# Delta rule's triangular inverse: 8x8 diagonal blocks solved by forward substitution on VectorE, heads planned as three interleaved lists, and the B and C pieces moved in between

## The chip, the cores and the metric

The kernel runs on one core of one Trainium2 chip. The metric is the device time of one execution in microseconds (us). The engines are called by the profile's names: PE is TensorE, PEld its weight loads, DVE VectorE, ACT ScalarE, POOL GpSimd, SP SyncE (here it only issues DMAs).

## What is computed

Two layers of a hybrid trunk on 1024 frames of width 1024, all in fp32. Each layer normalizes x, projects it once, sends the columns to three groups of heads (gated DeltaNet, Mamba-2 SSD, retention), projects their outputs back and adds. The change is in the DeltaNet group (4 heads of 128). The part of the reference that matters, for one chunk:

```
a_low = einsum('bihd,bjhd->bhij', k * beta, k) * decay * strict      # strictly lower triangular
sol   = triangular_solve(a_low + eye, [v * beta, k * beta * exp(gcum)], lower=True)
v_new = u - w @ S                      # u, w: the two halves of sol
o     = (q * exp(gcum)) @ S + ((q @ k.T) * decay) @ v_new
S     = S * exp(glast) + (k * exp(glast - gcum)).T @ v_new
```

The kernel takes chunks of 128 frames instead of 64 and so needs the inverse of a 128x128 unit triangular matrix for every chunk and head.

## The kernel before, in words

**Work and its parts.** The sequence is cut in halves of 512 frames (`HALF`); with two layers this makes four parts (`p` = 0 to 3, `PARTS`), each of four chunks (`NT`). In a part the input projection runs over 26 pieces of 256 columns (`PIECES`), each in two halves. A half is eight TensorE slices; products are taken in three fp32r passes (w_hi with hT_hi, w_low with hT_hi, w_hi with hT_lo), so a slice is three 512-wide matmuls for the pieces that pass through the convolution (`gdn`, `bc`, `sx`) and six 256-wide ones for the gates and the retention pieces. In parts 0 and 2 the weights are loaded and split into their high and low part on the chip (ACT L1954, POOL L2231) and kept in HBM; parts 1 and 3 load the split copies.

**The inverse.** For each head `h` the kernel forms aT (the scaled Gram matrix times the decay, for four chunks at once), starts from X = I minus the pairs on the diagonal (`gdn_gram`: three passes of DVE over 512 columns, L1675 to L1677), and then doubles the size of the inverted diagonal blocks in levels 1 to 6. A level takes `gdn_p` (PE: aT times X; DVE L1713: mask) and `gdn_xx` (PE: XT times the masked product; DVE L1698, or L1701 in the last level: subtract), each in two steps `j` of two chunks. Levels 2 to 5 also transpose X on DVE (L1707). A matmul with fp32 operands shows as two records of PE.

**The recurrence.** `gdn_s`, `gdn_v`, `gdn_o` then walk over the four chunks with the state (L1721, L1726, L1736), and `gdn_fin1` to `gdn_fin3` normalize and gate the output. After the four heads come SSD (two groups) and retention (four heads), and the output projection in units (`out`).

**The order.** Nothing is dynamic: `make_plan` plays a clock forward with costs written by hand (`LINE` 224 ns for a 128-wide fp32 matmul, `SLICE` 705 ns, and so on) and writes one list of steps; each engine runs its instructions in the order of that list, behind semaphores. The planner draws from one list of mixing steps (`mixing_steps`: one head wholly after another, SSD, retention), one of projection steps (`front_steps`), the output units, and short side chains. A mixing step is put in when it is due; otherwise a projection slice fills PE. What may come when is in `known` and `frees`: the convolved columns of a head lie in one of two slots, and the pieces of head h + 2 may only be projected when `gdn_gram` of head h has read its slot.

**Buffers.** `wk` holds 12 tiles of 128x512; X, XT and PP (the masked product, which also serves as oq) are one tile each. PSUM: two banks for the projection, five in a ring for the mixing steps (`MIX_BANKS`), one for outputs.

## Time and profile before

| | us |
|---|---|
| median of 3 runs | 2177.64 |
| lowest, highest | 2175.47, 2180.8 |
| span of the profiled execution | 2179.0 |
| PE busy in it | 2125.8 (98%) |
| PEld, DVE, ACT, POOL busy | 1963.9, 1350.4, 887.6, 482.6 |

The profile gives the span of the profiled execution, from its first to its last instruction, and no separate time of that execution; the span lies inside the spread of the three runs, 1.4 us above their median. A busy share is an average over the whole span, and matmul records overlap each other, so PE's busy time is an upper mark of its work, and what a matmul costs in a full stream is read from the distance of the starts.

### The profile page before, as it was taken

The numbers are of one execution on the slowest core, as the hardware profiler recorded it, in microseconds if no ns is written. First come the engines' busy times: TensorE is split into PE (matmuls) and PEld (weight loads), VectorE is DVE, ScalarE is ACT, GpSimd is POOL, SyncE is SP. The second block draws the span as 40 slices with busy tenths as digits, with TensorE's granted clock in tenths as the row PEclk, the third lists the DMA queues.
The fourth block names the chain that finished last, engine by engine and source line by source line (L and its number), as shares of the span: only waits on it lengthen the run. The fifth ranks groups of instructions, "written<-read, shape, count | busy, mean of one in ns | idle before, by whom it ended". The sixth has DMA issues, their size and how long they took to land.

```text
span 2179.0 us, 39125 instructions
## 1 busy us (share of the span) xinstructions
PE 2125.8 (98%) x15396; PEld 1963.9 (90%) x15396; DVE 1350.4 (62%) x2692; ACT 887.6 (41%) x1779; POOL 482.6 (22%) x432
## 2 busy tenths in 40 slices
PE   7899999999999999999999999999999999999997
PEld 6788988999898898999989899899988988899997
DVE  5777767545578757624567776674556777564334
ACT  5445377332433345402353444763324333562011
POOL 3334332431000011100333334423300000110001
PEclk9999999999999999999999999999999999999999
DMA  6646465666533446544574447666764333583433
GB/s 241 202 161 229 170 225 190 225 227 253 196 136 113 139 155 228 198 155 157 184 248 163 177 175 269 227 229 242 251 214 162 119 116 127 183 279 134 156 138 146
DMA packets 98197, 410.88 MB, mean 189 GB/s; under 512 B 11168, under 2 KB 12256, under 8 KB 84192
## 3 DMA queue, kind: packets, MB, share of 16 engines
q1 hardware_dynamic: 97440, 407.98, 53.0%
q8 instruction: 124, 2.03, 0.4%
q10 hardware_dynamic: 576, 0.41, 0.1%
q14 instruction: 57, 0.47, 0.1%
HBM read 257.18 MB, written 151.16 MB: 187 GB/s over the span
## 4 chain that ended last, share of the span: by engine, by line
PE 75%; issue 3%; DVE 2%; ACT 2%; DMA 1%; POOL 0%; POOLq 0%; DVEq 0%; ACTq 0%
PE ps L1216 71%; PE ps L1219 3%; ACT wk L2105 1%; DMA wo_loaded<-in_w_out 0%; DMA wk<-cum_rows 0%; ACT L2044 0%; DVE slot L1594 0%; DVE acc L1813 0%; DVE wk L1672 0%; ACT wk L2107 0%; ACT wk L2096 0%; DVE wk L1675 0%; DVE wk L1743 0%; ACT wo_hi_odd L1979 0%; DVE wk L1676 0%
## 5 line engine op out<-in xcount | busy, mean ns | idle before, releaser
L1216 PE MATMUL ps<-w_hi,hT_hi 128*128 128x256 f32 x1792 | 526.2, 294 | 4.2 <-POOL w_low L2231 2.5
L1216 PE MATMUL ps<-w_low,hT_hi 128*128 128x256 f32 x1792 | 505.0, 282 | 0.0
L1216 PE MATMUL ps<-w_hi,hT_lo 128*128 128x256 f32 x1792 | 502.7, 281 | 0.0
L2231 POOL TENSOR_TENSOR w_low<-w_loaded,w_hi 128x512 fp32r<-128x512 f32 x208 | 285.7, 1392 | 429.8 <-ACT w_hi L1954 429.5
L1216 PEld LDWEIGHTS ps<-wk 128*128 128x128 f32 x2336 | 309.1, 191 | 51.5 <-issue 15.4
L1216 PE MATMUL ps<-wk 128*128 128x128 f32 (+2 forms) x2336 | 342.7, 282 | 9.6 <-DVE wk L1677 5.8
L1216 PEld LDWEIGHTS ps<-w_hi,hT_hi 128*128 128x128 f32 x1792 | 338.8, 189 | 9.3 <-POOL w_low L2231 4.0
L1216 PEld LDWEIGHTS ps<-w_low,hT_hi 128*128 128x128 f32 x1792 | 338.5, 189 | 2.9 <-issue 2.6
L1216 PEld LDWEIGHTS ps<-w_hi,hT_lo 128*128 128x128 f32 x1792 | 338.6, 189 | 0.0
L1216 PE MATMUL ps<-hT_hi,w_hi 128*128 128x512 f32 x768 | 331.1, 431 | 2.1 <-POOL w_low L2231 2.0
L1216 PE MATMUL ps<-hT_lo,w_hi 128*128 128x512 f32 x768 | 303.2, 395 | 0.0
L1216 PE MATMUL ps<-hT_hi,w_low 128*128 128x512 f32 x768 | 302.2, 393 | 0.0
L1216 PE MATMUL ps<-wo_parts,mixT_hi 128*128 128x256 f32 x960 | 272.6, 284 | 0.0
L1594 DVE SCALAR_TENSOR_TENSOR slot<-raw,par,slot 128x512 f32<-128x512 f32 x240 | 205.1, 857 | 29.9 <-ACT slot L2022 15.7
L1813 DVE TENSOR_TENSOR acc<-acc,ps 128x512 f32<-128x512 f32 x96 | 65.8, 687 | 236.3 <-PE ps L1216 236.0
L1216 PEld LDWEIGHTS ps<-wo_parts,mixT_hi 128*128 128x128 f32 x960 | 182.9, 191 | 3.5 <-issue 2.4
L1216 PEld LDWEIGHTS ps<-hT_lo,w_hi 128*128 128x128 f32 x768 | 144.9, 189 | 33.2
L1216 PEld LDWEIGHTS ps<-hT_hi,w_hi 128*128 128x128 f32 x768 | 146.1, 190 | 24.8 <-POOL w_low L2231 3.8
L1216 PEld LDWEIGHTS ps<-hT_hi,w_low 128*128 128x128 f32 x768 | 146.2, 190 | 20.8 <-issue 1.4
L1216 PE MATMUL ps<-wo_hi_odd,mixT_hi 128*128 128x256 f32 x480 | 141.7, 295 | 12.3 <-DVE wo_parts L1799 8.4
L1954 ACT ACTIVATE w_hi<-w_loaded 128x512 fp32r<-128x512 f32 x208 | 120.8, 620 | 60.1 <-DMA w_loaded<-in_w_in 60.1
L1216 PE MATMUL ps<-wo_hi_odd,mixT_lo 128*128 128x256 f32 x480 | 137.5, 287 | 0.0
(205 smaller groups left out, 3566.7 us busy)
## 6 DMA issues: line engine op xcount, KB each, us to landing
w_loaded<-in_w_in SPq DMA_DIRECT2D x104, 512.0 KB, 5.1
w_split<-w_hi SPq DMA_DIRECT2D x52, 1024.0 KB, 8.1
w_split<-w_low SPq DMA_DIRECT2D x52, 1024.0 KB, 10.1
w_hi<-w_split SPq DMA_DIRECT2D x104, 512.0 KB, 6.3
w_low<-w_split SPq DMA_DIRECT2D x104, 512.0 KB, 7.2
wo_loaded<-in_w_out SPq DMA_DIRECT2D x32, 512.0 KB, 4.2
wk<-cum_rows SPq DMA_DIRECT2D x32, 512.0 KB, 4.5
wo_split<-wo_parts SPq DMA_DIRECT2D x32, 512.0 KB, 9.0
```

Source lines behind the costliest of these rows:

```text
L1216: return nc.tensor.matmul(o, a, b, start=start, stop=stop)
L1219: return nc.tensor.transpose(o, a, ident)
L1594: stt(o, r[:, j:j + HALF], w[:, j:j + 1], o, ALU.mult, ALU.add).then_inc(S["conv_done"], 1)
L1813: empty(tt(o, o, b, ALU.add), s)
L1954: A(w_hi[:, n % W_RING, j * 512:(j + 1) * 512], wr[:, n % W_RING, j * 512:(j + 1) * 512], ACT.Copy)\
L2105: ins = A(LG[:, j * P:(j + 1) * P], LG[:, j * P:(j + 1) * P], ACT.Relu, scale=-1.0, bias=cum_s[:, c, HG * g + j:HG * g + j + 1])
L2231: tt(w_lo[at], wr[at], w_hi[at], ALU.subtract)\
```

## The change

Levels 1 and 2 of the doubling fall away. Instead the 8x8 diagonal blocks are inverted by forward substitution on VectorE (`gdn_base`): aT is masked to its diagonal blocks, the blocks are gathered by a reduction into an 8-column tile, eight stream shuffles copy each of its rows over the partitions of its block, seven steps of a multiply and a subtract build the columns, and the result is spread over the 128x128 tiles and transposed. The step is cut into pieces (`base_parts`), which the planner places one by one.

`gdn_turn` is split: the transposes of k and q stay, that of v and the q-k Gram matrix move into a new step `gdn_open`, which is now what frees the slot. XT and kdc get a second buffer; PP moves to the unused end of a slot. The mixing steps of DeltaNet become three lists, drawn from side by side: what comes before the inverse (`ahead_steps`), the inverse (`inverse_steps`), and the recurrence with everything after it (`mixing_steps`). The pieces are reordered: B and C pieces lie between the DeltaNet pieces, and the second SSD gates between its x pieces. Four constants of the planner change or are new.

```diff
+BASE = 8
+FIRST = BASE.bit_length() - 1
+NBLK = P // BASE
...
-PIECES = ([("gz", 0)] + [("gdn", i) for i in range(4)] + [("gz", 1)] + [("gdn", i) for i in range(4, N_GDN_PC)]
-          + [("bc", i) for i in range(N_BC)]
-          + [(k, g, i) for g in range(SG) for k, n in (("sx", N_SX), ("sz", N_SZ)) for i in range(n)]
+PIECES = ([("gz", 0), ("gdn", 0), ("gdn", 1), ("gdn", 2), ("bc", 0), ("gz", 1), ("gdn", 3), ("bc", 1), ("gdn", 4), ("gdn", 5),
+           ("sx", 0, 0), ("sx", 0, 1), ("sz", 0, 0), ("sz", 0, 1), ("sx", 1, 0), ("sz", 1, 0), ("sx", 1, 1), ("sz", 1, 1)]
...
+def base_parts():
+
+    copies = [("copy", range(i, min(i + 3, BASE))) for i in range(0, BASE, 3)]
+    columns = [("column", range(i, min(i + 2, BASE - 1))) for i in range(0, BASE - 1, 2)]
+    return [("mask", ()), ("sum", ()), *copies, *columns, ("spread", ()), ("turn", ())]
...
+def inverse_steps(p):
+
+    return [(name, p, h, k, j) for h in range(GH) for k in range(FIRST, LEVELS) for name in ("gdn_p", "gdn_xx") for j in range(2)]
...
+def ahead_steps(p):
+
+    out = []
+    for h in range(GH):
+        out += [("gdn_decay", p, h), ("gdn_turn", p, h), ("gdn_gram", p, h)]
+        out += [("gdn_base", p, h, j) for j in range(BASE_END + 1)]
...
-    out = [("gdn_decay", p, 0)]
+    out = []
     for h in range(GH):
-        out += [("gdn_turn", p, h), ("gdn_gram", p, h), ("gdn_x0", p, h)]
-        for k in range(1, LEVELS):
-            out += [(name, p, h, k, j) for name in ("gdn_p", "gdn_xx") for j in range(2)]
+        out += [("gdn_open", p, h), ("gdn_x0", p, h)]
         for c in range(NT):
             out += [("gdn_s", p, h, c), ("gdn_v", p, h, c), ("gdn_o", p, h, c)]
-            out += [("gdn_decay", p, h + 1)] * (c == 0 and h + 1 < GH)
...
+        elif k == "gdn_base":
+            part, cols = BASE_PARTS[r[1]]
+            if part in ("mask", "spread"):
+                mark("n", both(900, *after))
+            elif part == "sum":
+                mark("n", dve(900, *after))
+            elif part == "copy":
+                mark("n", dve(len(cols) * (230 + 2 * BASE), *after))
+            elif part == "column":
+                mark("n", dve(len(cols) * 2 * (150 + 2 * BASE), *after))
...
+        if k == "gdn_turn" and r[0] and ("gdn_x0", p, r[0] - 1) not in done:
+            return False
...
+                "gdn_open": lambda: half_after(p, AT["gdn", (3 * r[0] + 2) // 2], (3 * r[0] + 2) % 2) if ("gdn_turn", p, r[0]) in done else ("gdn_turn", p, r[0]),
+                "gdn_x0": lambda: ("gdn_fin3", p, r[0] - 2) if r[0] > 1 else None,
+                "gdn_s": lambda: ("gdn_fin1", p, r[0] - 1) if r[0] and r[1] == 0 else None,
+                "gdn_v": lambda: ("gdn_xx", p, r[0], LEVELS - 1, r[1] // 2),
+                "gdn_gram": lambda: ("gdn_p", p, r[0] - 1, LEVELS - 1, 1) if r[0] else None,
...
-                "gdn_p": lambda: ("gdn_fin1", p, r[0] - 1) if r[1:] == (1, 0) and r[0] else None,
+                "gdn_p": lambda: ("gdn_base", p, r[0], BASE_END),
...
+        inverse = inv[inv_at] if inv_at < len(inv) and known(inv[inv_at]) else None
+        if inverse and due(inverse) <= now + NEAR:
+            inv_at += 1
+            emit(inverse)
+            continue
+        ahead = pre[pre_at] if pre_at < len(pre) and known(pre[pre_at]) else None
+        if ahead and due(ahead) <= now + (AHEAD if ahead[0] == "gdn_base" else NEAR):
+            pre_at += 1
+            emit(ahead)
...
-OUT_WAIT = 1500
+OUT_WAIT = 2500
...
-KEEP = 4
+KEEP = 8
...
+AHEAD = 700
...
     if j < 4:
-        return ("gdn_gram", p, j)
+        return ("gdn_open", p, j)
...
+    if PIECES[i] == ("sx", SG - 1, N_SX - 1) and half == 1:
+        need += [("gdn_xx", p, GH - 1, LEVELS - 1, j) for j in range(2)]
...
-        X, XT, PP, bT0, kr, kdc, vb, bT1, aT, att, qr = (wk[:, i] for i in range(11))
-        oq = PP
+        X, XT0, oq, XT1, kr, kdc0, vb, kdc1, aT, att, qr = (wk[:, i] for i in range(11))
+        kdc = (kdc0, kdc1)
+        XTs = (XT0, XT1)
+        PP, more = (slot[:, i, 3 * HALF:4 * HALF].rearrange("p (c n) -> p c n", c=NT) for i in (1, 0))
+        cols_x, diag, step_t = (base[:, i] for i in range(3))
+        copies = [half.rearrange("p c n -> p (c n)").rearrange("p (j c n) -> p j c n", c=NT, n=BASE) for half in (X, more)]
+        copy_of = lambda j: copies[j // (P // BASE)][:, j % (P // BASE)]
         resid, vhat = wk[:, 11, 0:2], wk[:, 11, 2:4]
...
+                elif k == "gdn_base":
+                    h, j = s[2:]
+                    part, at = BASE_PARTS[j]
+                    if part == "mask":
+                        wait_emptied(dve, ("gdn_gram", p, h))
+                        chain(tt(blocks(X), blocks(aT), own_block, ALU.mult))
+                    elif part == "sum":
+                        nc.vector.tensor_copy(cols_x, over_rows(con[:, C_EYE:C_EYE + BASE]))
+                        chain(nc.vector.tensor_reduce(diag, X.rearrange("p c (b n) -> p c n b", n=BASE), mybir.AxisListType.X, ALU.add))
+                    elif part == "copy":
+                        for i in at:
+                            ins = nc.vector.stream_shuffle(copy_of(i).rearrange("p c n -> p (c n)"), diag.rearrange("p c n -> p (c n)"),
+                                                           [q // BASE * BASE + i for q in range(32)])
+                        chain(ins)
+                    elif part == "column":
+                        for i in at:
+                            n = BASE - 1 - i
+                            chain(tt(step_t[:, :, i + 1:], copy_of(i)[:, :, i + 1:], cols_x[:, :, i:i + 1].broadcast_to([P, NT, n]), ALU.mult))
+                            chain(tt(cols_x[:, :, i + 1:], cols_x[:, :, i + 1:], step_t[:, :, i + 1:], ALU.subtract))
+                    elif part == "spread":
+                        chain(tt(blocks(XTs[h % 2]), cols_x.unsqueeze(2).broadcast_to([P, NT, NBLK, BASE]), own_block, ALU.mult))
+                    else:
+                        nc.vector.transpose(X.rearrange("p c n -> p (c n)"), XTs[h % 2].rearrange("p c n -> p (c n)")).then_inc(S["gdn_xt"], 1)
...
-                    chain(tt(XT, aT, over_rows(con[:, C_LEV:C_LEV + P]), ALU.mult))
-                    chain(tt(XT, XT, over_rows(ident), ALU.add))
-                    nc.vector.transpose(X.rearrange("p c n -> p (c n)"), XT.rearrange("p c n -> p (c n)")).then_inc(S["gdn_xt"], 1)
...
+                        if m == 23:
+                            for j in range(2):
+                                wait_emptied(act, ("gdn_xx", p, GH - 1, LEVELS - 1, j))
...
+                    if h and c < 2:
+                        act.wait_ge(S["o_gated"], GH * p + h)
+                        act.wait_ge(S["o_squares"], 8 * p + h)
```

## Rows read from the trace of the kernel before

**Rows 1.** The page: busy time and share of each engine.

```profile
PE 2125.8 (98%) x15396; PEld 1963.9 (90%) x15396; DVE 1350.4 (62%) x2692; ACT 887.6 (41%) x1779; POOL 482.6 (22%) x432
```

**Rows 2.** The page: the chain that ended last, by engine.

```profile
PE 75%; issue 3%; DVE 2%; ACT 2%; DMA 1%; POOL 0%; POOLq 0%; DVEq 0%; ACTq 0%
```

**Rows 3.** The waits of PE: for whom, us in total, times, longest.

```profile
PE ps L1219 <- ACT wk L1932: 9.2, 1, 9.2
PE ps L1216 <- DVE wo_parts L1799: 8.4, 3, 4.2
PE ps L1216 <- DVE wk L1677: 5.8, 5, 3.9
PE ps L1216 <- POOL w_low L2231: 4.5, 6, 1.5
```

**Rows 4.** Ten-us windows: PE, PEld, DVE, ACT, POOL busy, granted clock, DMA share.

```profile
0.00:10.00 10.00, 0.82 (x4) 0.85 (x5) 1.37 (x2) 5.58 (x7) 1.68 (x8) 1.00 0.75 239
...
70.00:80.00 10.00, 7.02 (x26) 6.12 (x27) 7.34 (x15) 5.46 (x10) 6.63 (x7) 0.66 0.96 333
...
560.00:570.00 10.00, 7.11 (x45) 6.09 (x43) 1.44 (x2) 2.38 (x3) 0.00 (x0) 1.00 0.77 263
...
2170.00:2180.00 10.00, 0.00 (x0) 0.00 (x0) 5.02 (x4) 0.67 (x2) 2.78 (x3) 0.57 0.26 105
```

**Rows 5.** Windows over the DeltaNet stages of parts 0, 2 and 1; columns as in rows 4.

```profile
50.00:300.00 250.00, 241.56 (x1536) 213.14 (x1535) 183.95 (x373) 117.63 (x242) 95.33 (x74) 0.99 0.53 187
1100.00:1350.00 250.00, 247.76 (x1686) 225.21 (x1684) 180.38 (x374) 105.89 (x214) 86.43 (x72) 1.00 0.57 203
590.00:800.00 210.00, 209.06 (x1434) 189.34 (x1433) 157.77 (x372) 74.91 (x146) 19.11 (x18) 1.00 0.38 128
```

**Rows 6.** Timeline of PE, part 1: start us, us, what.

```profile
705.83 0.39 PE L1216 MATMUL ps<-hT_lo,w_hi 128*128 128x512 f32 x1
706.05 0.61 PE L1216 MATMUL ps<-wk 128*128 128x128 f32 x4
...
706.98 0.40 PE L1216 MATMUL ps<-hT_lo,w_hi 128*128 128x512 f32 x1
...
703.07 0.39 PE L1216 MATMUL ps<-hT_lo,w_hi 128*128 128x512 f32 x1
...
703.76 0.40 PE L1216 MATMUL ps<-hT_lo,w_hi 128*128 128x512 f32 x1
```

**Rows 7.** Groups of instructions on wk: busy, mean ns, idle before.

```profile
L1216 PE MATMUL ps<-wk 128*128 128x128 f32 x2048 | 297.8, 278 | 9.6 <-DVE wk L1677 5.8 <-DVE wk L1726 1.7 <-issue 0.9
L1216 PEld LDWEIGHTS ps<-wk 128*128 128x128 f32 x2336 | 309.1, 191 | 51.5 <-issue 15.4 <-DVE wk L1677 8.5 <-DVE wk L1726 4.4
```

**Rows 8.** Groups of DVE that go, or resemble what comes.

```profile
L1713 DVE TENSOR_TENSOR wk<-ps,con 128x256 f32<-128x256 f32 x192 | 76.8, 405 | 23.3 <-PE ps L1216 21.4
L1698 DVE TENSOR_TENSOR wk<-wk,ps 128x256 f32<-128x256 f32 x160 | 66.1, 418 | 42.8 <-PE ps L1216 40.3
L1707 DVE STREAM_TRANSPOSE wk<-wk 128x256 f32<-128x256 f32 x128 | 55.5, 433 | 0.0
L1675 DVE TENSOR_TENSOR wk<-wk,con 128x512 f32<-128x512 f32 x16 | 16.3, 1016 | 0.5
L1676 DVE TENSOR_TENSOR wk<-wk,con 128x512 f32<-128x512 f32 x16 | 13.8, 862 | 0.5
L1677 DVE STREAM_TRANSPOSE wk<-wk 128x512 f32<-128x512 f32 x16 | 11.4, 712 | 0.5
L1646 DVE TENSOR_REDUCE gss<-junk 128x4 f32<-128x512 f32 x16 | 11.0, 685 | 14.6 <-ACT junk L2054 14.6
L1571 DVE SCALAR_TENSOR_TENSOR wk<-wk 128x80 f32<-128x80 f32 x28 | 6.8, 242 | 1.0
L1755 DVE TENSOR_TENSOR ss<-ss,sc 128x4 f32<-128x4 f32 x16 | 2.6, 164 | 0.6
```

**Rows 9.** Timeline of PE at the first head of part 0.

```profile
72.98 2.07 PE L1216 MATMUL ps<-wk 128*128 128x128 f32 x8 [3.92 <-DVE wk L1677]
```

190 lines of the change are left out of this document (115 added, 75 removed).

## The prediction

> **What bounds the kernel now.** I read the page first, for the engine that carries the span: PE is busy for 2125.8 of 2179.0 us, DVE for 1350.4 (62%), nothing else for half of it [rows 1]. Then the chain that ended last: 75% of it is PE's own work, and no other engine holds more than 3% [rows 2]. So the kernel is a stream of TensorE instructions with 53 us of holes (2179.0 less 2125.8). Where the holes are, the waits and the short windows tell: the first 10 us, before x and the first weights are there; 9.2 us for the normalized x [rows 3]; the change of part near 565 us, where PE is busy for 7.11 of 10 us and waits for a split of output weights; the last 10 us, in which PE has nothing left [rows 4]. In the DeltaNet stages, where the change lies, PE is idle for 8.4 of 250 us in part 0, 2.2 of 250 in part 2, and 0.9 of 210 in part 1 (part 3 is the same to 0.1 us) [rows 5]. The long dependency chain of the inverse is therefore already covered by projection slices and output units nearly everywhere. A change is worth here what it takes from PE, and costs what it adds in holes.
>
> **What goes from PE.** Levels 1 and 2 are two levels x two kinds of step x two j = 8 steps a head, over 4 heads and 4 parts 128 steps, each of two fp32 matmuls (four records). The price of a step is read from a full stream: from one last matmul of a slice to the next takes 0.69 us without a step in between (703.07 to 703.76) and 1.15 us with one (705.83 to 706.98) [rows 6], so a step costs 0.46 us and 128 steps cost 58.9 us. I take 58 us, since starts are given to 0.01 us and the neighbouring slice takes 0.70. Nothing else of PE changes in amount: v's transposes and the second Gram product only move into `gdn_open`, the level-6 transposes stay, and the pieces are the same 26 in another order, each with the same matmuls.
>
> The busy time of the group of these matmuls would say more: 297.8 us for 2048 records [rows 7] is 145 ns each and 74 us for the 512 that go; but a record's time overlaps the next one's, so part of it returns as busy time of the neighbour. The Trainium skill ("Perfetto Trace Analysis", section Identifying the Most-Contended Engine) holds that the occupancy of matmuls is a poor measure of the headroom and asks for the share of the weight loads; by that the group is 309.1 us for 2336 records [rows 7], or 68 us for 512, and the loads' 90% of the span would promise 215 us of headroom. The trace does not bear out that headroom: a 512-wide matmul is spaced 0.23 us from the next and its load takes 0.19, so the loads can't fill the stretch. The sum goes by the spacing.
>
> **What goes from and comes to DVE.** Per head go: the three passes that set X up, 1.016 + 0.862 + 0.712 = 2.59 us; four masks of 0.405 and four subtractions of 0.418, 3.29; four transposes of 0.433 (the ones of level 2 and 3, since the lowest level needs none), 1.73 [rows 8]. Together 7.6 us. Per head come: the block mask, two operands in SBUF over 512 columns, like L1675 at 1.02; the small copy of 32 columns, between 0.164 (4 columns) and 0.242 (80 columns), taken as 0.2; the reduction of 512 columns, 0.685 as L1646; the spread, 0.86 to 1.02, taken as 0.95; the transpose, 0.71 [rows 8]: 3.6 us. Then 14 small operations on 4 to 28 columns, between 0.164 and 0.242 each, with some 0.04 us of idle before each as those rows have (0.6 us over 16, 1.0 over 28): 14 x 0.22 = 3.1 us. The shuffles have no row. Below, they are the smallest DVE instruction, 0.164; above, a 256-column transpose, 0.433, whose lanes are permuted the same way but over eight times the columns; the two transposes (256 columns 0.433, 512 columns 0.712) give 1.09 ns a column and 0.154 fixed, so 0.19 for 32 columns, and I take that: 8 x 0.19 = 1.5 us, bounds 1.3 and 3.5. Together 8.2 us, so DVE gains 0.6 us a head or 10 us over 16 heads, within 0.4 and 2.6 us a head. It stays under PE: in the stage of part 1 DVE is busy for 157.8 of 210 us [rows 5], and after the change it would be some 160 of 195. The cost is therefore set to nothing, with PE's own stream as its cover; without that cover it would be 8.2 us a head on PE.
>
> A page speaks of one more item, which no row here has. The Trainium skill ("Vector Engine (DVE) Microarchitecture Reference", section 3.8) says that a shuffle's lane choice is loaded by an instruction of its own and persists. Eight different choices a head would be eight more instructions, at the smallest row 1.3 us a head; the sum to the end would not move.
>
> **Waits added, and who stands behind them.** (a) PE waits for the transposed X of the base (the count `gdn_xt`) before level 3, with projection slices queued behind. The planner gives the base 0.9 + 0.9 + 8 x 0.246 + 14 x 0.166 + 0.9 + 0.72 = 7.7 us against my 8.2; 0.5 us late at 16 heads is 8 us if nothing is in between, but each of the ten parts is placed by its own due time and 0.7 us ahead, so I charge 1 us in all. At the first head of part 0 PE waits for this point now, 3.92 us [rows 9], and the granted clock of that window is 0.66 [rows 4]; I keep that wait. (b) ACT waits for the gating of head h - 1 before it evicts the q product, with projection evictions behind it; ACT already squares that gated product itself in an earlier step, so it costs nothing, and 1.4 us x 12 heads on ACT (41% busy, [rows 1]) if not. (c) The last half of the second SSD x pieces waits for the fourth head's inverse, in the planner, in ACT and so in the weight ring; loads of the next two pieces on SP's queue stand behind. By the list this lies seven pieces (some 79 us of slices at 16 x 0.7) after the last DeltaNet piece, more than the inverse needs. (d) POOL's copies of k and q move with `gdn_open`; weight splits of the next piece stand behind them, as now. The DMAs are the same in number and size but for a shorter load of constants.
>
> **What the new order gives.** Two B/C pieces (four halves) can now be projected while a slot is still held, and the base and transposes of head h + 1 run beside the recurrence of head h. That can only close holes. In the DeltaNet stages there are 8.4 + 2.2 + 0.9 + 1.0 = 12.5 us of them [rows 5]; I take back 4, and leave those of the start, of the changes of part and of the end.
>
> **Sum.** 2179.0 - 58 + 1 - 4 = 2118 us for the span of a profiled execution; the median of the runs was 1.4 us below the span shown, so 2116.6, rounded to 2116 us, a gain of 2.8%.
>
> **The rivals.**
> *Part of it comes back as waits in parts 0 and 2.* There the weights are split on the chip, and PE already waits 4.5 us for w_low [rows 3]; POOL is busy for 95 of 250 us [rows 5]. If the piece stream in these two parts can't run faster, half of the 58 us is lost: 2116 + 29 = 2145. Against it: 95 of 250 is far from full.
> *The holes close as well.* The three lists cover all 12.5 us of the stages rather than 4, and some 5 us at the changes of part (2.9 us of idle in the one window of [rows 4]): 2116 - 8.5 - 5 = 2102 or less. For it: the new order touches just these places; against it: PE's wait there for output weights is of another kind.
> *Slower: the base is late at every head.* DVE runs it in the list's order between convolutions and evictions, PE stands at `gdn_xt`, and what was a covered cost is on the path. The gain is 58 / 16 = 3.6 us a head, so it decides from a base that is 3.6 us later than PE's turn, 11.3 us against the planned 7.7. With the whole 8.2 us uncovered the time would be 2116 + 16 x 8.2 = 2247; with 4.5 us a head, 2188. For it: DVE is 75% busy in these stages, and the first head shows such a wait. Against it: shuffles at their upper bound add only 2.0 us a head, 2148.
> *No change.* The removed work had been hidden: it would need holes of PE behind it, and 0.9 us in 210 leaves no room.
>
> **How the numbers follow.** The forecast holds with 0.60, from 2104 to 2130 (charge (a) up to 8 us, 74 or 58 us removed, the holes kept or half closed). The closed holes have 0.14 (2090 to 2104), the lost half or shuffles at their bound 0.18 (2130 to 2165), no change 0.03, slower 0.05. The range from 2095 to 2150 leaves out a part of each side, together under 0.2. Runs of this kernel lie within 0.3% (6.5 us) of each other, about what a measurement can tell from no change. Faster than 2171: 0.60 + 0.14 + 0.18 = 0.92; within 0.3%: 0.03; slower: 0.05.
>
> **What would show it.** 512 fewer wk matmul records; PE busy near 2066 to 2068 with 48 to 52 us of holes; the DVE groups at 1350 + 10 = 1360 us; shuffles near 0.19 us each, a base of 8 to 9 us a head; no wait of PE for the base's transpose above 6 us in all. The prediction is wrong if PE's idle time in the stages of parts 0 and 2 grows beyond 15 us each, if shuffles take over 0.43 us, or if PE's waits for the base are 1 us or more at most heads.

## The result: 19 us gained where 61 were forecast

| | before | after |
|---|---|---|
| median of 4 runs, us | 2179.22 | 2160.27 |
| lowest, highest | 2175.47, 2181.87 | 2156.42, 2162.2 |
| span of the profiled execution | 2179.0 | 2160.4 |
| mean granted clock | 0.994 | 0.984 |

The ratio is 0.9916, with a 95% interval from 0.9904 to 0.9927. The kernel is faster, but the time is above the forecast of 2116 us and above the range that ended at 2150.

The page of the kernel after: busy time by engine [rows 1].

```profile
PE 2080.1 (96%) x14884; PEld 1918.3 (89%) x14884; DVE 1368.3 (63%) x3012; ACT 888.7 (41%) x1777; POOL 483.2 (22%) x432
```

The 512 records are gone (15396 to 14884). DVE's busy time grew by 18 us, where 10 were forecast. What misses is on PE. Its holes, the span less the busy time, were 53.2 us and are 80.3 us: 27 more. Its busy time should have gone from 2125.8 to 2066.9 with the 58.9 us of the removed steps, and is 2080.1: the same matmuls were busy for 13 us more. The two together are all that is missing from the 58.9: 58.9 - 27.1 - 13.2 = 18.6 us, which is the difference of the spans. So two things have to be found: where 27 us of new holes are, and why matmuls became longer.

The waits of PE in the kernel after; columns as in [rows 3].

```profile
PE ps L1301 <- POOL w_low L2357: 19.4, 11, 5.8
PE ps L1301 <- DMA wo_parts<-wo_split: 10.7, 1, 10.7
PE ps L1304 <- ACT wk L2052: 9.2, 1, 9.2
PE ps L1301 <- DVE wo_parts L1919: 7.1, 2, 4.0
PE ps L1301 <- DVE wk L1846: 7.0, 7, 2.4
```

The wait for the normalized x (9.2) and that for output weights by DVE (7.1, was 8.4) are old. New are 15 us more for w_low, which was 4.5 [rows 3], one wait of 10.7 us for output weights by DMA, and 7.0 us for L1846, a step of the recurrence. There is no wait of PE for the base's transpose (L1799) at all: the rival that put the whole base on PE's path did not come true in that form.

The three stages of [rows 5] in the kernel after; columns as there.

```profile
50.00:300.00 250.00, 227.60 (x1344) 197.57 (x1343) 186.59 (x450) 116.66 (x241) 91.62 (x70) 0.94 0.50 176
1100.00:1350.00 250.00, 240.00 (x1617) 217.76 (x1616) 193.90 (x462) 116.64 (x236) 90.15 (x74) 0.99 0.58 203
590.00:800.00 210.00, 209.91 (x1439) 191.75 (x1438) 161.16 (x451) 76.24 (x145) 18.49 (x23) 1.00 0.47 159
```

PE's idle time is 22.4 of 250 us in part 0 (8.4 before), 10.0 in part 2 (2.2 before) and 0.1 of 210 in part 1 (0.9 before). So 22 us of the new holes lie in these two windows, in the parts that split their weights on the chip, and in part 0 the granted clock fell from 0.99 to 0.94 with them. With the 10.7 us of the end these are all the new holes, and more. Most of what part 2 adds is not in the work on the heads, though: 5.5 of its 7.8 us are one wait at 1336, at the first SSD chunk.

```profile
1341.49 0.58 PE L1301 MATMUL ps<-w_hi,hT_hi 128*128 128x256 f32 x1 [5.52 <-POOL w_low L2357]
```

The w_hi that this w_low is split from stands on ACT behind that chunk's exponentials, which themselves wait 3.7 us for rows in transfer.

The same change, by whole parts. The first normalized tile of a part marks its start; the timeline of DVE, before (L1543) and after (L1642), for parts 1, 2 and 3.

```profile
509.08 0.69 DVE L1543 TENSOR_TENSOR hT_hi<-ps,par 128x512 fp32r<-128x512 f32 x1 [3.29 <-PE ps L1219]
1042.98 0.69 DVE L1543 TENSOR_TENSOR hT_hi<-ps,par 128x512 fp32r<-128x512 f32 x1 [3.29 <-PE ps L1219]
1576.35 0.69 DVE L1543 TENSOR_TENSOR hT_hi<-ps,par 128x512 fp32r<-128x512 f32 x1 [3.29 <-PE ps L1219]
```

```profile
517.12 0.69 DVE L1642 TENSOR_TENSOR hT_hi<-ps,par 128x512 fp32r<-128x512 f32 x1 [3.29 <-PE ps L1304]
1032.54 0.69 DVE L1642 TENSOR_TENSOR hT_hi<-ps,par 128x512 fp32r<-128x512 f32 x1 [3.29 <-PE ps L1304]
1560.64 0.69 DVE L1642 TENSOR_TENSOR hT_hi<-ps,par 128x512 fp32r<-128x512 f32 x1 [3.29 <-PE ps L1304]
```

Each part lost 58.9 / 4 = 14.7 us of PE work. Part 0 nevertheless got 8.0 us longer (509.1 to 517.1). Part 1 took 533.9 and takes 515.4: 18.5 shorter, all of its share and a little more. Part 2 took 533.4 and takes 528.1: 5.3 shorter. Part 3, to the end of the span, took 602.7 and takes 599.8: 2.9 shorter, and it holds the wait of 10.7 us.

**Where PE stands in part 0.** Two stretches of the timeline of the kernel after. The first is the first head, with POOL and PE.

```profile
81.33 1.65 POOL L2299 TENSOR_TENSOR rs<-gss,con 128x8 f32<-128x8 f32 x1 [3.49 <-DVE gss L1756]
...
84.06 2.50 POOL L2357 TENSOR_TENSOR w_low<-w_loaded,w_hi 128x512 fp32r<-128x512 f32 x2
...
85.38 0.79 PE L1301 MATMUL ps<-hT_hi,w_hi 128*128 128x512 f32 x1 [5.80 <-POOL w_low L2357]
85.97 0.63 PE L1301 MATMUL ps<-hT_hi,w_low 128*128 128x512 f32 x1
```

POOL works in the order of the list. Its next split (L2357) stands behind three operations of the first head (this one and two copies), and the first of these waits 3.49 us for DVE's sums. PE waits 5.80 us for the split. After the hole the 512-wide matmuls take 0.63 us instead of 0.40: the clock is at the lower of its two levels. The second stretch is the recurrence of an early head of part 0, PE alone.

```profile
147.97 0.71 PE L1301 MATMUL ps<-st_g,wk 128*128 128x128 f32 x4 [0.74 <-DVE st_g L1856]
149.16 0.46 PE L1301 MATMUL ps<-wk 128*128 128x128 f32 x2 [0.48 <-issue]
151.18 1.22 PE L1301 MATMUL ps<-wk 128*128 128x128 f32 x4 [1.56 <-DVE wk L1846]
152.47 1.22 PE L1301 MATMUL ps<-st_g,wk 128*128 128x128 f32 x4
```

There is no projection slice between these steps, so each wait, two of them for DVE and one for nothing that the profile shows, is a hole of 0.5 to 1.6 us, and from 151 on the same four records take 1.22 us where they took 0.71. The list has nothing else to give here: the next pieces need a slot that frees only with `gdn_open` of a head whose step stands behind this recurrence.

The list that `make_plan` writes shows how far this goes. From the first `gdn_v` to the last `gdn_o` of a head, the kernel before has 11, 38, 10 and 11 projection slices for the four heads of part 0. The kernel after has 10, none, 17 and 10, and the 10 of the first head all stand before its last six steps. In parts 1 to 3 every head has 12 to 18. So the recurrence runs bare at two heads of sixteen, both in part 0 and the first of them from its third chunk on: these are the stretches from 140 to 157 and from 185 to 201, and PE is idle in them for 7.8 of 33 us. Ten-us windows show the two places of the stretches above, and the end of the kernel; columns as in [rows 4].

```profile
80.00:90.00 10.00, 4.62 (x13) 3.68 (x14) 9.15 (x20) 4.25 (x8) 5.23 (x6) 0.66 0.59 220
150.00:160.00 10.00, 8.10 (x33) 7.25 (x34) 6.53 (x20) 2.28 (x3) 2.30 (x3) 0.53 0.06 23
...
2100.00:2110.00 10.00, 4.96 (x42) 4.76 (x40) 2.61 (x4) 0.00 (x0) 0.00 (x0) 0.99 1.02 404
2110.00:2120.00 10.00, 4.38 (x20) 4.38 (x21) 0.00 (x0) 0.00 (x0) 0.00 (x0) 0.50 0.40 158
```

In the window from 150 PE is 81% busy at a granted clock of 0.53. These windows give an estimate of what the clock took: over all windows of 10 us, PE's busy time times what is missing from a clock of 1.00 (here 8.10 x 0.47 = 3.8 us) sums to 8.1 us before and 20.2 us after. That is 12 us more, against the 13 us by which the matmuls are longer. Before, four windows in which PE works had a clock below 0.97, now ten have. In part 0 the sum went from 2.4 us (one window, [rows 4]) to 11.6 us: 9 us more, which with the 14 us of holes in its stage makes 23 us, and part 0 has lost 14.7 + 8.0 = 22.7. Of the 11.6 us, 10.0 are in the four windows at the two bare recurrences (150 to 170 and 190 to 210). With their 7.8 us of holes they make 17.8 us, most of what part 0 lost.

**The base itself.** DVE's groups in the kernel after; the first is one that stood before too, for comparison.

```profile
L1745 DVE TENSOR_REDUCE gss<-junk 128x4 f32<-128x512 f32 x16 | 10.9, 682 | 21.7 <-ACT junk L2177 21.6
...
L1785 DVE TENSOR_REDUCE base<-wk 128x32 f32<-128x512 f32 x16 | 18.5, 1158 | 0.0
...
L1788 DVE STREAM_SHUFFLE wk<-base 128x32 f32<-128x32 f32 x128 | 17.5, 187 | 0.0
L1784 DVE COPY base<-con 128x32 f32<-128x32 f32 x16 | 3.8, 239 | 0.0
L1794 DVE TENSOR_TENSOR base<-wk,base 128x28 f32<-128x28 f32 (+6 forms) x112 | 24.9, 222 | 2.0
L1795 DVE TENSOR_TENSOR base<-base 128x28 f32<-128x28 f32 (+6 forms) x112 | 27.8, 248 | 3.9
L1797 DVE TENSOR_TENSOR wk<-base,con 128x512 f32<-128x512 f32 x16 | 12.1, 753 | 0.3
L1799 DVE STREAM_TRANSPOSE wk<-wk 128x512 f32<-128x512 f32 x16 | 11.3, 704 | 0.1
L1782 DVE TENSOR_TENSOR wk<-wk,con 128x512 f32<-128x512 f32 x16 | 11.4, 713 | 0.0
```

A shuffle takes 187 ns, as forecast (0.19). Mask and spread were dearer in the sum than they are (0.71 and 0.75 against 1.02 and 0.95), the reduction was cheaper in it (0.685 against 1.158). With the small copy (L1784) all of it is 18.5 + 17.5 + 3.8 + 24.9 + 27.8 + 12.1 + 11.3 + 11.4 = 127.3 us over 16 heads, 8.0 us a head against 8.2. What was not forecast is the time from its beginning to its end. One base on the timeline of DVE:

```profile
92.76 1.20 DVE L1785 TENSOR_REDUCE base<-wk 128x32 f32<-128x512 f32 x1
93.99 3.58 DVE L1693 SCALAR_TENSOR_TENSOR bc<-raw,par,bc 128x512 f32<-128x512 f32 x2
...
100.27 0.75 DVE L1693 SCALAR_TENSOR_TENSOR bc<-raw,par,bc 128x512 f32<-128x512 f32 x1
...
102.65 0.17 DVE L1794 TENSOR_TENSOR base<-wk,base 128x28 f32<-128x28 f32 x1
...
109.48 0.71 DVE L1799 STREAM_TRANSPOSE wk<-wk 128x512 f32<-128x512 f32 x1
```

Convolutions (L1693) of 0.75 to 1.8 us each stand between its pieces. From the reduction to the end of the transpose are 17.4 us. From DVE's first step on a head's Gram product (L1770) to the start of the transpose of X it is 18.9, 19.2, 24.3 and 19.2 us in the mean of parts 0 to 3, and from 14 to 34 us at single heads; it was 3.7, 2.9, 2.9 and 2.9 before, when levels 1 and 2 still followed it on PE. This is called the elapsed time of the base below.

### The profile page after: what moved, and what is told of

It reads as the page before. It is cut to its first block, busy times and chain, and to the rows that moved or that the text cites. A ratio compares the mean times of both kernels' runs of the same rounds, so it can differ in the third digit from the quotient of the medians.

```text
span 2160.4 us, 38435 instructions
## 1 busy us (share of the span) xinstructions
PE 2080.1 (96%) x14884; PEld 1918.3 (89%) x14884; DVE 1368.3 (63%) x3012; ACT 888.7 (41%) x1777; POOL 483.2 (22%) x432
## 4 chain that ended last, share of the span: by engine, by line
PE 84%; issue 4%; DVE 4%; DMA 4%; ACT 2%; POOL 1%; SPq 0%; POOLq 0%; DVEq 0%; ACTq 0%
PE ps L1301 80%; PE ps L1304 4%; DMA wk<-cum_rows 1%; DMA wo_loaded<-in_w_out 1%; DMA wo_split<-wo_parts 1%; POOL w_low L2357 1%; DVE base L1795 1%; DMA w_split<-w_low 0%; ACT wk L2231 0%; DVE slot L1693 0%; DVE base L1794 0%; DMA wk<-in_x 0%; DMA w_loaded<-in_w_in 0%; DVE acc L2011 0%; DVE wk L1846 0%
## 5 line engine op out<-in xcount | busy, mean ns | idle before, releaser
L1301 PE MATMUL ps<-w_hi,hT_hi 128*128 128x256 f32 x1792 | 529.7, 296 | 11.8 <-POOL w_low L2357 10.0
L2357 POOL TENSOR_TENSOR w_low<-w_loaded,w_hi 128x512 fp32r<-128x512 f32 x208 | 285.7, 1390 | 411.1 <-ACT w_hi L2074 411.0
L1301 PE MATMUL ps<-hT_hi,w_hi 128*128 128x512 f32 x768 | 323.0, 421 | 9.4 <-POOL w_low L2357 9.4
L1693 DVE SCALAR_TENSOR_TENSOR slot<-raw,par,slot 128x512 f32<-128x512 f32 x240 | 206.8, 865 | 32.6 <-ACT slot L2143 15.0
L1301 PE MATMUL ps<-wk 128*128 128x128 f32 (+2 forms) x1312 | 205.5, 290 | 12.5 <-DVE wk L1846 7.0
L1301 PEld LDWEIGHTS ps<-wk 128*128 128x128 f32 x1312 | 177.4, 195 | 37.7 <-issue 14.4
L1301 PE MATMUL ps<-wo_hi_odd,mixT_hi 128*128 128x256 f32 x480 | 139.5, 291 | 17.8 <-DMA wo_parts<-wo_split 10.7
L1301 PE MATMUL ps<-wo_hi,mixT_hi 128*128 128x256 f32 x480 | 135.8, 283 | 1.4 <-DVE mixT_lo L1905 1.4
```

The costliest lines, as they stand in the source:

```text
L1301: return nc.tensor.matmul(o, a, b, start=start, stop=stop)
L1693: stt(o, r[:, j:j + HALF], w[:, j:j + 1], o, ALU.mult, ALU.add).then_inc(S["conv_done"], 1)
L2357: tt(w_lo[at], wr[at], w_hi[at], ALU.subtract)\
```

## The experiments

Thirteen kernels ran. Those with k4 in the name carry the first edit, `KEEP = 4`, as well, and are compared with keep4 (2147.98 us). The ratio is to runs of the kernel before taken beside each kernel.

| run | median, us | ratio to before | 95% interval |
|---|---|---|---|
| keep4 | 2147.98 | 0.9853 | 0.9837 to 0.9869 |
| oldorder | 2209.71 | 1.0136 | 1.0120 to 1.0151 |
| serial | 2222.32 | 1.0191 | 1.0176 to 1.0206 |
| base4 | 2201.32 | 1.0097 | 1.0082 to 1.0112 |
| k4_addwork | 2204.55 | 1.0119 | 1.0104 to 1.0134 |
| k4_baseshort | 2134.88 | 0.9803 | 0.9788 to 0.9817 |
| serial_old | 2206.65 | 1.0124 | 1.0109 to 1.0139 |
| k4_base2 | 2205.47 | 1.0123 | 1.0105 to 1.0141 |
| k4_ahead1500 | 2160.38 | 0.9921 | 0.9904 to 0.9937 |
| k4_pool0 | 2152.69 | 0.9878 | 0.9861 to 0.9896 |
| k4_poolact0 | 2146.10 | 0.9845 | 0.9830 to 0.9860 |
| k4_six | 2163.22 | 0.9918 | 0.9903 to 0.9933 |
| k4_six3000 | 2144.62 | 0.9840 | 0.9824 to 0.9856 |

### The end: output units kept back

```diff
-KEEP = 8
+KEEP = 4
```

> The changed kernel with one constant set back: KEEP is 4 again instead of 8, so the planner holds back fewer output units for the end. Theory E (the end): in the changed kernel all eight units of the third group come after the last projection slice, the unit that PE waits for 10.7 us (at 2105) is loaded behind 12 other transfers; with 4 kept back it is loaded in time, as before the change, where that wait was 1.7 us. Expected: 2160 - 9 = 2151 us, the 10.7 us wait gone. Rival: the wait is only PE's spare time seen at another place (the last head's chain and the x rows set the end); then the time stays within 2157 to 2163 us and another wait of about 10 us appears after 2080 us.

2147.98 us, 12.3 below the kernel after. The cause can be read on the queue. SP's queue in the kernel after, at the last weights of the output projection (SPq: time spent issuing):

```profile
2093.64 1.93 SPq L1182 DMA_DIRECT2D wk<-x_mid  x4
2095.68 0.37 SPq L1259 DMA_DIRECT2D w_hi<-wo_split  x1
...
2099.76 0.50 SPq L1260 DMA_DIRECT2D w_low<-wo_split  x1
2100.30 0.50 SPq L1253 DMA_DIRECT2D wo_hi_odd<-wo_split  x1
2100.90 0.40 SPq L1272 DMA_DIRECT2D wo_parts<-wo_split  x1
```

and where PE waits for them:

```profile
2115.62 0.58 PE L1301 MATMUL ps<-wo_hi_odd,mixT_hi 128*128 128x256 f32 x1 [10.66 <-DMA wo_parts<-wo_split]
```

The planner keeps up to `KEEP` output units back as filler. It counts steps of the list, two to a unit. With eight, all four units of the third group stand behind the last slice, and the weights of the fourth unit are issued behind four loads of x rows and eight for the tail, into a DMA share of 1.02 in the window from 2100; PE stands for 10.66 us and then works at a clock of 0.50 in the next window. In keep4 SP issues the eight loads for the tail from 2084.36 to 2088.25, these weights 3.0 us later, and the x rows only behind them. The first line of the weights, and the waits:

```profile
2091.27 0.32 SPq L1253 DMA_DIRECT2D wo_hi_odd<-wo_split  x1
...
PE ps L1301 <- POOL w_low L2357: 20.1, 14, 5.8
...
PE ps L1301 <- DMA wo_parts<-wo_split: 1.8, 1, 1.8
```

The wait has shrunk from 10.7 to 1.8 us, which is 8.9 of the 12.3; the window at a clock of 0.50 is gone as well, an estimated 2.2 us more (4.38 x 0.50). Parts 0 to 2 are as they were, within 1.6 us. `OUT_WAIT`, which the change moves from 1500 to 2500, was not run by itself beside the kernel after.

### Is the removed work worth its price?

Put back as much matmul work as was taken out: each product of level 3 is issued three times.

```diff
-                        i = mm(b[:, c * P:(c + 1) * P], aT[:, 2 * j + c, :], X[:, 2 * j + c, :])
+                        for _ in range(3 if lv == FIRST else 1):
+                            i = mm(b[:, c * P:(c + 1) * P], aT[:, 2 * j + c, :], X[:, 2 * j + c, :])
...
+                        for _ in range(3 if lv == FIRST else 1):
```

> The kernel keep4 (the changed one with KEEP = 4, 2148 us) with the removed PE work put back and nothing else: in level 3, gdn_p and gdn_xx each issue their matmuls three times into the same bank, so PE has again 8 x 16 steps of two fp32 matmuls more, with the order of the steps, the waits and DVE untouched. What PE's amount alone is worth: by the step price of 0.46 us 58.9 us if PE is the bound everywhere (2207 us); if it is the bound only in parts 1 and 3 and stands waiting in parts 0 and 2, about 30 us (2178 us). The repeats also lengthen the chain of each head by 3.6 us, which is inside both numbers.

2204.55 us, 1.0119 against 0.9853: 0.0266 x 2179 = 58 us for 128 steps, or 0.45 us a step, beside the 0.46 read from the spacing [rows 6]. The page of the run:

```profile
PE 2133.4 (97%) x15396; PEld 1972.4 (90%) x15396; DVE 1369.4 (62%) x3012; ACT 888.9 (40%) x1777; POOL 483.6 (22%) x432
```

PE's busy time is 57.6 us above keep4's 2075.8. The first term of the sum was right in mechanism and size. Even keep4, with its holes, pays for each step in full, so its holes are not places where this work could go.

### The parts of the change one by one

The pieces in their old order, all else after:

```diff
-PIECES = ([("gz", 0), ("gdn", 0), ("gdn", 1), ("gdn", 2), ("bc", 0), ("gz", 1), ("gdn", 3), ("bc", 1), ("gdn", 4), ("gdn", 5),
-           ("sx", 0, 0), ("sx", 0, 1), ("sz", 0, 0), ("sz", 0, 1), ("sx", 1, 0), ("sz", 1, 0), ("sx", 1, 1), ("sz", 1, 1)]
+PIECES = ([("gz", 0)] + [("gdn", i) for i in range(4)] + [("gz", 1)] + [("gdn", i) for i in range(4, N_GDN_PC)]
+          + [("bc", i) for i in range(N_BC)]
+          + [(k, g, i) for g in range(SG) for k, n in (("sx", N_SX), ("sz", N_SZ)) for i in range(n)]
```

> The changed kernel with the pieces in the order of before (B and C pieces behind all DeltaNet pieces). Theory F (front stuck): a head's slot is freed only when the head before it has run its recurrence, and in that time PE has slices only if pieces that need no slot lie between; the B and C pieces are these. Without them the waits of parts 0 and 2 grow by up to 22 us each, PE's work unchanged: 2180 to 2205 us. Rival A (amount only, the step of the prediction): the order is worth the 4 us of holes it closed, 2160 to 2166 us.

2209.71 us, 49 above the kernel after, and above the range expected. Heads one after another:

```diff
-        if k == "gdn_turn" and r[0] and ("gdn_x0", p, r[0] - 1) not in done:
+        if k == "gdn_turn" and r[0] and ("gdn_fin1", p, r[0] - 1) not in done:
```

> The changed kernel with the heads one after another: gdn_turn of head h (and with it Gram matrix and base) is placed only after gdn_fin1 of head h - 1. Theory L (latency): the base takes 15 to 24 us from the Gram matrix to the transposed X, because its parts stand between convolutions in DVE's order, against 3 us before the change; uncovered by the recurrence of the head before, each of 16 heads gets about 10 us longer, and the projection slices don't suffice in parts 0 and 2: 2185 to 2215 us. Rival A (amount only): the lists add nothing where PE has slices to fill with, 2160 to 2166 us.

2222.32 us, 62 above, and again more than expected. Both at once, with `KEEP = 4` and `OUT_WAIT = 1500`: nearly the old plan with the base in place of levels 1 and 2.

> The 8x8 base alone: the changed kernel with one head after another, the pieces in the order of before, KEEP = 4 and OUT_WAIT = 1500 as before. Theory L: the base takes PE work of 58 us away and lengthens each head by the elapsed time of the base in DVE's order (20 us or more against 3) less two levels; without the lists and the B and C pieces to cover it, it costs more than it saves: 2200 to 2235 us. Rival A (amount only): 2179 - 58 = 2121, with 10 us of holes 2131 us.

2206.65 us. This kernel still draws the steps of a head from three lists and has the new buffers, so it is the nearest run to the base alone, not the base alone. It is 27 us slower than the kernel before, although PE has 59 us less to do: 86 us went back. Its page and waits of PE:

```profile
PE 2112.0 (96%) x14884; PEld 1932.8 (88%) x14884; DVE 1391.4 (63%) x3012; ACT 890.3 (40%) x1779; POOL 484.3 (22%) x432
PE ps L1302 <- POOL w_low L2358: 19.5, 15, 5.8
PE ps L1302 <- DVE wk L1800: 15.3, 3, 6.2
PE ps L1302 <- DVE wk L1847: 12.3, 23, 1.5
```

Here the base's transpose (L1800) is a wait of PE: three of up to 6.2 us, as the rival of the late base had it. The holes are 92.7 us, 39 above the old (53.2), and the busy time of 2112 us is 45 above 2066.9. Half of this is the clock: the sum over the windows is 30.2 us, 22 above before. The rest I put down to records that stand alone and no longer overlap a neighbour, which was not tested. Now the reverse, the new plan with all six levels:

```diff
-BASE = 8
+BASE = 2
```

> The kernel keep4 with 2x2 diagonal blocks: all six levels are there again (PE's work as before the change), the base has 2 shuffles and one column step and costs DVE about 4.2 us a head. So it is the lists and the new order of the pieces without the saving on PE. If the lists and the order are worth something by themselves: below 2179 us. If they only pay for the base: 2148 + 58.9 = 2207 us, less the smaller base (up to 11 us), 2196 to 2207 us.

2205.47 us, 57 above keep4 and 26 above before, in the range for lists that only pay for the base. It does the same matmul work as k4_addwork (15396 records each), and both stand within 1 us of one another. So the new lists and order, without the saving, cost 26 us against the old plan; in this is the 2x2 base, which runs in six pieces on DVE and keeps the head waiting longer than the old start of X did. The change is thus two things that are each slower nearly alone (+27 and +26 us) and 31 us faster together. Neither can be priced by itself and added.

The pair k4_base2 and k4_addwork says more. Their elapsed times of the base are 11.8, 13.0, 14.4 and 11.9 us against 19.0, 19.2, 24.3 and 19.2, and yet they take the same time (k4_base2 has two more levels behind its base, so the comparison is not quite even, and it is 5.3 us shorter in part 0 and 8.3 longer in parts 1 and 2). So nothing here shows that in the new plan the base's elapsed time as such sets the time. And the 26 us that this plan costs with all its levels is as much as keep4 falls short of the 58.9.

The base with 4x4 blocks, beside the kernel after:

```diff
-BASE = 8
+BASE = 4
```

> The changed kernel with 4x4 diagonal blocks: level 2 comes back (64 steps of 0.46 us, 29 us of PE work), and the base loses 4 shuffles and 4 column steps of two operations, about 2.4 us of DVE a head, nothing else. Rival A (amount only): 2160 + 29 = 2189 us. Theory L: half of the latency that the 8x8 base adds and PE's work trade one against the other, so the time grows by less than the work: 2168 to 2182 us.

2201.32 us. It is 41 us above the kernel after, where half of the saved work, 29 us, was put back; no theory foretold the other 12. Its waits for output weights that DVE joins are 11.4 us instead of 7.1, and those for w_low 17.2 instead of 19.4; these are no explanation for 12 us, and the cause stayed open. Both theories had the time too low.

### What the base's work on DVE costs

The eight shuffles and seven column steps are left out, so the diagonal blocks are not inverted; mask, sum, spread and transpose stay.

```diff
-                    elif part == "copy":
+                    elif part in ("copy", "column"):
+                        pass
+                    elif part == "copy":
```

> The kernel keep4 without the eight shuffles and the fourteen column operations of each base (so the diagonal blocks are left as the identity; that part of the computation is left out), in the same order of steps. Takes about 4.6 us of DVE from each head, 73 us in all. Theory L (the latency of the base on DVE makes PE wait in the chip's own time): the holes of part 0 between 80 and 260 us shrink, 2148 - 15 = 2133 us or less. Theory P (the holes were put there by the list: the planner found nothing to fill with, and the chip keeps that list however fast DVE is): at most 4 us, 2144 to 2149 us.

2134.88 us, 13.1 below keep4 (11 us by the ratios), near the 15 of theory L and far from the 4 of theory P. DVE lost 71 us of busy time, so less than a fifth of it was being paid for. The lengths of the parts tell where: part 0 is 7.0 us shorter than in keep4 (511.1 against 518.1), part 2 4.2 us (523.3 against 527.5), parts 1 and 3 within 1.3 us. In parts 1 and 3 the base's work is hidden; in parts 0 and 2 4.4 us a head of it is worth 1 to 1.8 us a head. Their elapsed times fell by 3.2 and 1.5 us a head only. The list is the same as in keep4, so the order of the steps and its two bare recurrences stay: PE still waits for w_low (19.3 us), and its waits for L1846 fell from 7.1 to 3.4 us.

Fewer pieces: the copies in one piece and the columns in one, and then also a longer lead in the planner.

```diff
-    copies = [("copy", range(i, min(i + 3, BASE))) for i in range(0, BASE, 3)]
-    columns = [("column", range(i, min(i + 2, BASE - 1))) for i in range(0, BASE - 1, 2)]
+    copies = [("copy", range(BASE))]
+    columns = [("column", range(BASE - 1))]
...
-AHEAD = 700
+AHEAD = 3000
```

> The kernel keep4 with the base in six pieces instead of eleven: all eight shuffles in one piece of the list, all seven columns in another. The same instructions; only what may stand between them changes. Theory Q (each piece waits its turn in DVE's list, so the elapsed time of the base goes by their number): from the Gram product to the transposed X 13 to 16 us instead of 19 to 24, and the time falls below keep4's 2148 us, to 2135 to 2145 us. Rival P (the planner's whole order changes, and blocks of 2 to 3 us on DVE hold up evictions and convolutions): the elapsed time falls but the kernel gets slower, 2150 to 2170 us.

> As k4_six, and AHEAD = 3000: a piece of the base may be placed up to 3 us before PE's clock, so the pieces stand one behind another in DVE's list. Theory Q: elapsed 10 to 13 us, 2130 to 2142 us. Rival P: 2150 to 2170 us, unrelated to the elapsed time.

The six pieces alone gave 2163.22 us, 15 above keep4, as the rival had it, though the elapsed time hardly fell; with `AHEAD = 3000` 2144.62, 3.4 below it and the least of all kernels that do the whole work, though the intervals of the two overlap. The lead alone, in the eleven pieces:

```diff
-AHEAD = 700
+AHEAD = 1500
```

> The kernel keep4 with AHEAD = 1500 instead of 700: the planner places a part of the base up to 1.5 us ahead of PE's clock. The same instructions in another order. Theory P (the order that the planner arrives at decides, and a small constant changes it everywhere): the time moves by more than 10 us, most likely up, to 2160 to 2185 us. Rival: the base gets shorter in elapsed time and the time stays or falls, 2140 to 2150 us.

2160.38 us, 12 above keep4, inside the range of theory P. The elapsed time of the base, in the mean of parts 0 to 3: keep4 18.9, 19.2, 24.3, 19.2 us; six 17.7, 18.2, 25.1, 18.2; six3000 18.8, 16.9, 13.9, 17.8; ahead1500 20.6, 17.3, 22.4, 19.2. six3000 takes it down by 10 us in part 2, and that part takes 518.0 us instead of 527.5, as the theory of the latency wants. But part 0 is 10.6 us shorter too, at the elapsed time of keep4, and part 3 is 11.3 us longer at a shorter one; and six is a little quicker than keep4 at three of four and yet slower as a kernel. So the elapsed time is not the measure of the whole: each edit of a constant also deals the list anew, and the time moved by up to 15 us with it. What goes with part 0 in six3000 is the filler: by its list the first two heads have 33 and 21 slices in their recurrences where keep4 has 10 and none, and the estimate of what the clock took in part 0 is 5.5 us against 13.4. That is read from one list, and no run changed the filler alone.

### The weights of parts 0 and 2

POOL takes the next two splits before the first head's `gdn_turn`, so that they don't stand behind its wait; and then ACT and POOL do so before the first step `ssd_exp` too. The list of these engines is passed through this function:

```diff
+def split_first(plan, kinds, most):
...
+        if s[0] in kinds and s[1] % 2 == 0 and s[2:] in ((0, ), (0, 0)):
+            ahead = [j for j in range(i + 1, min(i + 9, len(plan))) if plan[j][0] == "split" and j not in taken][:most]
+            out += [plan[j] for j in ahead]
...
-            for s in plan:
+            for s in split_first(plan, ("gdn_turn", ), 2):
```

> The kernel keep4 (2148 us) with one change of order on POOL alone: at the first head of parts 0 and 2 the weight splits that stand in the next eight places of the list run before gdn_turn's power and gdn_open's copies instead of behind them (in part 0 two of them, in part 2 none stands there). Theory W (PE waits 5.8 us at 80 us because two w_low splits stand behind a power that waits for DVE and ACT): that wait falls to about 1.5 us and the time of keep4 by 3 to 6 us, to 2142 to 2145 us. Rival: the late piece was late from its load, and the time is given back at the next wait: 2147 to 2149 us.

> As k4_pool0, and at the first SSD chunk of parts 0 and 2 the splits of the next eight places run before the exponentials, on ACT and on POOL. In the changed kernel PE waits 5.5 us at 1336 for a w_low whose w_hi stands on ACT behind the exponentials, which wait 3.7 us for rows in transfer. Theory W: another 3 to 5 us, 2138 to 2142 us. Rival: the exponentials get late by what the splits gain, and nothing is left: within 2 us of k4_pool0.

The first gave 2152.69 us, not faster than keep4 (4.7 above it), and PE waits as much for w_low as before: 19.8 us in 12 waits against 20.1 in 14. The hole at 80 us went as the theory had it, from 5.8 to 1.8 us, but new waits stand behind it, 1.1 us at 93 and this one:

```profile
97.02 0.58 PE L1315 MATMUL ps<-w_hi,hT_hi 128*128 128x256 f32 x1 [3.29 <-POOL w_low L2371]
```

So the split's place behind the head's wait did make that hole, and freeing it gained nothing, as the rival said. The second gave 2146.10, between the two expectations. Its waits of PE:

```profile
PE ps L1315 <- POOL w_low L2371: 13.9, 10, 3.3
```

6 us less wait for w_low, and 6.6 us less time than k4_pool0 (0.9845 against 0.9878, 7 us), though only 1.9 less than keep4, which is within the intervals. By the one comparison such a wait is worth its length, by the other a third of it, so its price stayed open. The long wait of part 2, at 1336, fell from 5.4 to 2.1 us. A cheaper split, which would say how much of all this is the weights, was not tried.

### The parts in all runs

Length of parts 0 to 3 in us, each from the first normalized tile of one part to that of the next (the last to the end of the span):

| | 0 | 1 | 2 | 3 |
|---|---|---|---|---|
| before | 509.1 | 533.9 | 533.4 | 602.7 |
| after | 517.1 | 515.4 | 528.1 | 599.8 |
| keep4 | 518.1 | 513.8 | 527.5 | 587.2 |
| k4_addwork | 530.4 | 529.7 | 540.3 | 600.4 |
| k4_baseshort | 511.1 | 515.1 | 523.3 | 586.6 |
| k4_poolact0 | 516.8 | 515.0 | 525.4 | 587.5 |
| k4_six3000 | 507.5 | 517.7 | 518.0 | 598.5 |
| k4_base2 | 525.1 | 534.7 | 543.6 | 600.1 |
| serial_old | 530.5 | 527.1 | 551.1 | 596.0 |

In keep4 parts 1 and 3 are 20.1 and 15.5 us shorter than before, their full 14.7; part 0 is 9.0 longer and part 2 5.9 shorter. 24 us are lost in part 0 and 9 in part 2, 33 in all, less the 6 that parts 1 and 3 gain beyond their share: 26, the difference of 58.9 and 32.5. In k4_six3000 22 to 26 matmul records have moved out of part 0 and out of part 2 into the part behind, so its lengths differ from keep4's by some 3 us of moved work too.

## Why the prediction was wrong, step by step

**What goes from PE: right.** 58 us were charged, and 58 is what the same number of steps costs when it is put back. By the Trainium skill ("Perfetto Trace Analysis", section Identifying the Most-Contended Engine), which asks for the share of the weight loads beside the rate of arithmetic, the kernel with holes would by its loads have had room, since they fill 89% of the span. This trace does not bear it out: more work cost its full length. The trace's spacing was the right measure, as the prediction chose.

**DVE's cost "set to nothing, with PE's own stream as its cover": wrong, the first of two steps that failed.** The size of the base was right, 8.0 us a head against 8.2. But busy time was used for latency. DVE takes its steps in the list's order; the base is cut in eleven pieces (the prediction counted ten), and between them stand convolutions of 0.75 to 1.8 us, so that 8.0 us of work lasts 19 to 24 us in the mean of a part. PE's stream covers this only where it has other work that is allowed. In parts 1 and 3 it has; there the cost is nothing, as foretold. In parts 0 and 2 a part of it shows: 11 to 13 us go when shuffles and columns go, where the sum had nothing. It does not show as a wait for the base. In part 0 it shows one step further on, where two heads' recurrences run with no slice between their steps; that the cover for the base is what used these slices up is argued from the list, not shown. The diagnostic that I named, PE's idle time above 15 us in the stages of parts 0 and 2, was met in part 0 (22.4) and not in part 2 (10.0); the other, a wait of PE for the base, gave a false all-clear.

**"That can only close holes": wrong, the second.** I took back 4 us for the new order. Without the saving, lists and order cost 26 us (k4_base2), nearly the whole of what keep4 lacks; the prediction did not count the slices in the list, where the bare recurrences of part 0 stand to be seen. With the base they are worth a lot, 49 us for the order and 62 for the interleaving, but that is against a base that gives back 86 us in nearly the old plan. I had noted that the rival of a late base decides from 3.6 us a head and gave it 0.05; in serial_old, where little covers the base, it is what happens, 5.4 us a head lost (86 / 16) and the kernel 27 us slower. The order is what turned that rival into a gain of 1%; in the prediction it was listed as a small extra.

**A term that was not there.** The diff moves `KEEP` from 4 to 8, and I gave it no price. It cost 12.3 us at the end: a known list, and the last window's queue could have been followed. With it corrected the kernel would have come in at 2148, inside the range by 2 us and still 32 above the forecast; that would have been luck, since both steps above would have been wrong all the same.

**The clock was not in the sum.** I counted a hole at its length. In the kernel after, holes grew by 27 us and the lower clock in the windows around them took, by the estimate above, 12 us more, nearly half of their length again. [Rows 4] had shown it, 0.66 around the one hole at 73 us.

**The waits.** (a) PE waits little for the base's transpose, as charged. (b) ACT's busy time did not change (887.6 to 888.7), and the gated product is no wait of PE after; it is one of 19.4 us in serial (for DVE's gate, four times). (c) No wait for the last SSD pieces is among PE's. (d) "as now" was wrong: POOL's splits behind the head's steps are part of a wait that went from 4.5 to 19.4 us. The first of the two runs showed that freeing one place can move the wait on; which resource sets it was not settled.

**The rival that fits** is the first, "part of it comes back as waits in parts 0 and 2", with 2145 us and 0.18. Its place was right in both parts, and in keep4 its size too (26 us lost where it had 29). That nearness is partly luck: it had only the stream of weights, while the larger loss of part 0 is in recurrences that the plan leaves bare. What it had not at all was the 12 us of the end.

**What is open.** 26 us between keep4's 32.5 and 58.9. By PE's account they are 17.5 us of holes and 9 us of longer matmuls (busy 2075.8 against 2066.9; the sum over the windows gives 9.6 us for the clock), and by place they are in parts 0 and 2. 11 to 13 us go when shuffles and columns go. In part 0 of the kernel after, waits for w_low went from 2.6 to 13.4 us, those with DVE's steps of the recurrence or nothing visible behind them from nothing to 8.0 us, with most of the clock's loss beside them, while 4.9 us of waiting for the first X went away. How the 26 us divide between waits for w_low, the recurrence without filler and the chance order of the list the runs don't say: nearly every edit that could part them was itself a new order, worth up to 15 us either way.

## What to carry to other kernels

Price a moved operation by two numbers, its busy time and the time from its first to its last instruction in its engine's order; a chain of dependent steps has to be covered for the second, and where the bound engine's filler is itself limited, the cover has to be shown stage by stage. Where a program writes the order, the filler between dependent steps can be counted in the list before anything runs: two bare recurrences go with most of what part 0 lost here. Where a diff brings a mechanism together with the plan that hides it, neither is "extra": each nearly alone was 26 to 27 us slower here and the two together 31 us faster. Constants of a planner are edits like others: each gets a line in the sum, and one that changes what stands at the end of a queue is followed there.

## What the hardware showed that was not expected

- A reduction from 128x512 to 128x32 whose reduced axis is strided took 1.158 us, one from 128x512 to 128x4 over a contiguous axis 0.682: the same elements read, 1.7 times the time. Whether the stride or the eight times as many sums cost it no run parts.
- The shuffles of 32 columns overlap: 0.18 us each by the record, and 0.11 us from start to start (97.50, 97.61, 97.72). The Trainium skill ("Vector Engine (DVE) Microarchitecture Reference", section 3.8) says that the lane choice is loaded by an instruction of its own; the trace agrees and gives its price, 128 of them in 1.7 us, 13 ns each.
- Most two-operand column steps of 4 to 28 columns in this base take 0.17 to 0.19 us, but single ones take 1.2 us, with nothing on the page that says why:

```profile
104.36 1.26 DVE L1794 TENSOR_TENSOR base<-wk,base 128x12 f32<-128x12 f32 x1
...
106.90 1.21 DVE L1794 TENSOR_TENSOR base<-wk,base 128x8 f32<-128x8 f32 x1
```
